# Routing from the unnormed residual: logits scaled afterwards, the first task's rows gathered raw, the stored rows normed by GpSimd

## What is computed

```
h2 = rmsnorm(xs, norm2_g[l]) * (1.0 + sc2) + sh2
xs = xs + g2 * channel_mixer(h2, l, ...)

# channel mixer of layer 1
logits = (h @ w_router[i]).astype(F32)
top_v, top_i = lax.top_k(logits, TOP_K)
top_w = jax.nn.softmax(top_v, axis=-1)
gates = jnp.sum(jax.nn.one_hot(top_i, N_EXP) * top_w[..., None], axis=-2)
for e in range(N_EXP):
    y = y + gates[..., e:e + 1] * swiglu(h, w_ex_gate[i, e], w_ex_up[i, e], w_ex_down[i, e])
```

## Time and profile before

| | us |
|---|---|
| median of three runs | 1532.15 (1530.58 to 1533.17) |
| the profiled execution | 1533.48 |
| its span, first to last instruction | 1531.4 |

### The profile page before, as it was taken

One profiled execution on the slowest core, in us unless ns is written; L12 is line 12 of the kernel. 1 busy time (PEld: TensorE's weight loads), 2 busy tenths in 40 slices (PEclk: granted clock), 3 DMA queues, 4 the chain that ended last, 5 costly groups with the idle time before them and its releaser, 6 DMA issues.

```text
span 1531.4 us, 22089 instructions
## 1 busy us (share of the span) xinstructions
PE 1484.0 (97%) x8652; PEld 1308.3 (85%) x8652; DVE 937.7 (61%) x1077; ACT 786.7 (51%) x896; POOL 53.6 (4%) x54
## 2 busy tenths in 40 slices
PE   5999999999999999999999999998999999999997
PEld 4788969799899999997889696998888888888875
DVE  3542265555554254346522755556798898988988
ACT  4434354453432242235333544435778778787875
POOL 0100000000000000001000000000000000000002
PEclk8999999999999999999999999999999999999999
DMA  9754365467753544265333554535899999999994
GB/s 329 245 179 152 110 221 165 157 205 244 261 154 96 150 130 126 90 220 169 121 116 111 165 165 138 165 121 186 298 376 389 376 374 374 381 386 376 376 378 165
DMA packets 236026, 342.33 MB, mean 224 GB/s; under 512 B 8629, under 2 KB 156766, under 8 KB 235694
## 3 DMA queue, kind: packets, MB, share of 16 engines
q1 hardware_dynamic: 227392, 313.32, 59.9%
q0 software_dynamic: 6496, 24.69, 4.4%
q10 hardware_dynamic: 2062, 3.24, 0.6%
HBM read 325.74 MB, written 15.47 MB: 223 GB/s over the span
## 4 chain that ended last, share of the span: by engine, by line
PE 89%; DVE 5%; ACT 3%; DMA 1%; issue 1%; ACTq 0%; DVEq 0%; SPq 0%
PE ps L689 26%; PE ps L691 25%; PE ps L690 25%; PE ps L706 2%; DVE wlo L2142 2%; PE ps L887 1%; PE ps L921 1%; PE ps L905 1%; ACT whi L1575 1%; PE ps L1119 1%; PE ps L748 1%; ACT ebuf L1483 1%; PE ps L785 1%; PE ps L716 1%; DMA raw<-in_w_ada_dram 0%
## 5 line engine op out<-in xcount | busy, mean ns | idle before, releaser
L689 PE MATMUL ps<-hhi,whi 128*128 128x384 f32 x824 | 276.6, 336 | 0.3 <-DVE hidlo L2239 0.3
L691 PE MATMUL ps<-hhi,wlo 128*128 128x384 f32 x824 | 275.3, 334 | 0.0
L690 PE MATMUL ps<-hlo,whi 128*128 128x384 f32 x824 | 275.3, 334 | 0.0
L1763 DVE TENSOR_TENSOR wlo<-raw,whi 128x2048 fp32r<-128x2048 f32 x66 | 151.0, 2289 | 179.9 <-ACT whi L1317 168.3
L2142 DVE TENSOR_TENSOR wlo<-raw,whi 128x2048 fp32r<-128x2048 f32 (+1 forms) x81 | 179.0, 2227 | 27.4 <-ACT whi L1575 26.9
L1575 ACT ACTIVATE whi<-raw 128x2048 fp32r<-128x2048 f32 (+1 forms) x81 | 150.5, 1868 | 49.4 <-PE ps L691 47.8
L2142 DVE TENSOR_TENSOR wlo<-mraw,whi 128x2048 fp32r<-128x2048 f32 (+2 forms) x81 | 160.7, 1992 | 18.1 <-ACT whi L1575 17.6
L689 PE MATMUL ps<-whi,xgh 128*128 128x512 f32 (+1 forms) x432 | 164.7, 381 | 6.2 <-DVE wlo L2142 3.7
L1575 ACT ACTIVATE whi<-mraw 128x2048 fp32r<-128x2048 f32 (+2 forms) x81 | 136.6, 1686 | 53.2 <-PE ps L691 52.9
L691 PE MATMUL ps<-whi,xgl 128*128 128x512 f32 (+1 forms) x432 | 161.4, 374 | 0.0
L690 PE MATMUL ps<-wlo,xgh 128*128 128x512 f32 (+1 forms) x432 | 161.3, 373 | 0.0
(11 more groups left out here) (343 smaller groups left out, 2498.2 us busy)
## 6 DMA issues: line engine op xcount, KB each, us to landing
raw<-in_w_ada_dram SPq DMA_DIRECT2D x64, 512.0 KB, 5.4
raw<-in_w_ex_up_dram SPq DMA_DIRECT2D x27, 1024.0 KB, 6.7
raw<-in_w_ex_down_dram SPq DMA_DIRECT2D x27, 1024.0 KB, 5.1
raw<-in_w_gate_dram SPq DMA_DIRECT2D x48, 512.0 KB, 4.6
raw<-in_w_in_dram SPq DMA_DIRECT2D x44, 512.0 KB, 5.9
raw<-in_w_ex_gate_dram SPq DMA_DIRECT2D x18, 1024.0 KB, 7.3
mraw<-in_w_ex_gate_dram SPq DMA_DIRECT2D x18, 1024.0 KB, 7.8
mraw<-in_w_ex_down_dram SPq DMA_DIRECT2D x18, 1024.0 KB, 8.6
```

Of the source, the lines that this page charges most:

```text
L689: pe.matmul(out, s[0], m[0], start=first, stop=False, **kw)
L690: pe.matmul(out, s[0], m[1], start=False, stop=False, **kw)
L691: return pe.matmul(out, s[1], m[0], start=False, stop=last, **kw)
L1763: dve.tensor_tensor(wlo[:, n % RING, :], raw[:, n % RING, :], whi[:, n % RING, :].bitcast(F32), ALU.subtract).then_inc(lo_done, 1)
```

## The change

Six things change; the sums stay the same up to rounding.

1. The logits. In the output projection VectorE multiplies the router's weights by the modulation's scale, once for each kind of token (`wr2`). TensorE multiplies the residual `xT` with them as soon as its channel groups are there (`raw_logits`), and sums the squares between. The reciprocal root `rcol` is applied to the turned logits by VectorE, which also adds the shift's part (`shlog`). That part is made by 16 matmuls in front of the third slot of the output projection.
2. `mean_squares(3)`, `root(3)` in its old place, `normalise(3)` and `modulate(3)` are gone: neither the spreading of the root nor `macc` is made.
3. TensorE turns the residual (`residual_turned`) behind the logits and ahead of the places of the tokens; the turning of `macc` (L1079), its copies (L1740) and ScalarE's store (L1743) are gone.
4. `first_rows` gathers from `xtok2`, with `gat` holding rcol instead of 1; block 0 goes to PSUM banks of its own. One more matmul spreads which slots hold context tokens (`prompt`).
5. ScalarE scales and shifts the gathered rows as latent ones (`hmod`), VectorE adds the context rows with their scale and the difference of the shifts (`first_modulated`); high and low parts are made from `hmod`.
6. GpSimd makes the normed rows for the later tasks from `xtok2` by nine instructions of 128x1024 (times rcol, times scale, plus shift) and stores them to `h2d`. Scale and shift rows reach it as the gate's do: four more transposes, one more copy and store (`modrow`, `m2d`), four more broadcast loads. ScalarE's wait for this store is now in `expert_task`, in front of the copy to `ehh`.

The core of the diff:

```diff
@@ gpsimd
+            pool.wait_ge(rows_in, 16 * 7)
+            pool.wait_ge(rstd_ready, 2 * DEPTH)
+            pool.wait_ge(x2_tr, BLK)
+            for b in range(BLK):
+                v = int(b == 0)
+                pool.wait_ge(x2_ev, b + 1)
+                pool.tensor_scalar(h2tok[:, b, :], xtok2[:, b, :], rcol[:, 1, b:b + 1], None, ALU.mult).then_inc(h2_rows, 1)
+                pool.wait_ge(h2_rows, 3 * b + 1)
+                pool.tensor_tensor(h2tok[:, b, :], h2tok[:, b, :], murow[:, v, :], ALU.mult).then_inc(h2_rows, 1)
+                pool.wait_ge(h2_rows, 3 * b + 2)
+                pool.tensor_tensor(h2tok[:, b, :], h2tok[:, b, :], shrow[:, v, :], ALU.add).then_inc(h2_rows, 1)
+            pool.wait_ge(h2_rows, 3 * BLK)
+            pool.dma_start(h2d.rearrange("(b p) d -> p b d", p=P), h2tok[:, :, :]).then_inc(h2_out, 16)
@@ tensor: out_projection, in front of the third slot
+                            pe.transpose(ps[0:KD, 6, v * P:(v + 1) * P], mods[:, 1, SH2:SH2 + KD, v], ident)
+                            pe.transpose(ps[0:KD, 6, (2 + v) * P:(3 + v) * P], amul[:, 1, 1, :, v], ident)
                             mm = pe.transpose(ps[0:KD, 7, v * P:(v + 1) * P], mods[:, 1, G2:G2 + KD, v], ident)
                         mm.then_inc(g2_tr, 1)
+                        pe.wait_ge(wrout_in, 16)
+                        for v in range(2):
+                            for k in range(KD):
+                                mm = pe.matmul(ps[:, 5, v * N_EXP:(v + 1) * N_EXP],
+                                               mods[:, 1, SH2 + k, v:v + 1].to_broadcast([P, P]), wrout[:, k, 0:N_EXP],
+                                               start=(k == 0), stop=(k == KD - 1))
+                        mm.then_inc(sh_mm, 1)
@@ tensor: router
+                def raw_logits(k):
                     g = 32 * (k % 4)
-                    mm = pe.matmul(ps[g:g + 32, 7, 0:T], wrout[:, k, :], macc[:, k, :], start=(k < 4), stop=(k >= 4),
-                                   tile_position=(0, g))
+                    for v, t in ((0, slice(P, T)), (1, slice(0, P))):
+                        mm = pe.matmul(ps[g:g + 32, 7, t], wr2[:, v, k, :], xT[:, k, t], start=(k < 4 and v == 0),
+                                       stop=(k >= 4 and v == 1),
+                                       tile_position=(0, g))
+                    return mm
...
+                for k in range(6):
+                    raw_logits(k)
+                pe.wait_ge(wr2_ready, 2)
+                pe.wait_ge(sqs_done, SQS[3])
+                squares_part(0, False)
+                pe.wait_ge(res_done, 15)
+                raw_logits(6)
+                pe.wait_ge(sq_done, SQ0[3] + 4)
+                squares_part(1, False)
+                pe.wait_ge(res_done, 16)
+                raw_logits(7).then_inc(rt_rows, 1)
+                pe.wait_ge(sq_done, SQ0[3] + 5)
+                squares_part(2, True).then_inc(ssq_done, 1)
...
+                pe.wait_ge(rstd_ready, 2 * DEPTH)
                 for b in range(BLK):
-                    pe.wait_ge(x2_ev, b + 1)
...
+                    residual_turned(b)
@@ tensor: first_rows
-                pe.wait_ge(h2_ev, BLK)
+                pe.wait_ge(x2_ev, BLK)
+                pe.matmul(ps[:, 4, 0:P], ones[:, :], prompt[:, :], start=True, stop=True)
@@ scalar: expert_task, experts
+                        act.wait_ge(h2_out, 16)
                         act.activation(ehh[:, 4 * c:4 * c + CHUNKS[c] // P, :].rearrange("p k c -> p (k c)"),
...
-                act.wait_ge(h2_out, 16)
                 for h in range(2):
                     act.wait_ge((half_rows, xg_tr)[h], 1)
+                    for k in range(4 * h, 4 * h + 4):
+                        act.activation(hmod[:, k, :], ps[:, 2 + h, (k % 4) * P:(k % 4 + 1) * P], ACT.Identity,
+                                       scale=amul[:, 1, 1, k, 0:1], bias=mods[:, 1, SH2 + k, 0:1]).then_inc(half_mod, 1)
@@ vector: router
+                for b in range(BLK):
+                    x = dve.scalar_tensor_tensor(lg[:, b, :], ps[:, 7, T + b * N_EXP:T + (b + 1) * N_EXP], rcol[:, 1, b:b + 1],
+                                                 shlog[:, int(b == 0), :], ALU.mult, ALU.add)
...
+                dve.tensor_scalar(prompt[:, :], slot1[:, :], posx[:, 0, 0:1], None, ALU.is_equal)
                 for b in range(BLK):
-                    x = dve.tensor_scalar(gat[:, b, :], slotc[:, P:2 * P], 1.0, posx[:, b, 0:1], ALU.add, ALU.is_equal)
+                    x = dve.tensor_scalar(gat[:, b, :], slot1[:, :], posx[:, b, 0:1], rcol[:, 1, b:b + 1], ALU.is_equal, ALU.mult)
...
+                first_modulated(0)
...
-                for h in range(2):
-                    first_low(h)
+                first_low(0)
+                first_modulated(1)
+                first_low(1)
...
+            def first_modulated(h):
+                dve.wait_ge(half_mod, 4 * h + 4)
+                ks = range(4 * h, 4 * h + 4)
+                for k in ks:
+                    x = dve.scalar_tensor_tensor(hmod[:, k, :], ps[:, h, (k % 4) * P:(k % 4 + 1) * P], amul[:, 1, 1, k, 1:2],
+                                                 hmod[:, k, :], ALU.mult, ALU.add)
+                link(x)
+                for k in ks:
+                    x = dve.scalar_tensor_tensor(hmod[:, k, :], ps[:, 4, 0:P], shdiff[:, k:k + 1], hmod[:, k, :], ALU.mult, ALU.add)
+                x.then_inc(h_mod, 1)
```

More of the change, by code:

```diff
@@ L254, in prefix_step_kernel @@
         gat = at("gat", T, oraw_at + 4096, shape=[BLK, P])
+        slot1 = at("slot1", P, oraw_at + 2048)
+        prompt = at("prompt", P, oraw_at + 2560)
+        shlog = at("shlog", 2 * N_EXP, oraw_at + 3072, shape=[2, N_EXP])
+        shdiff = at("shdiff", KD, oraw_at + 3200)
         ehh = at("ehh", KF * P, oraw_at + 5632, F32R, [KF, P])
@@ L1060, in router, with squares_part @@
             def router():
-                pe.wait_ge(wrout_in, 16)
-                for k in range(KD):
-                    if k % 2 == 0:
-                        pe.wait_ge(chain_m, 8 * 3 + k + 2)
-                        pe.wait_ge(mod_done, 4 * 3 + k // 2 + 1)
-                    g = 32 * (k % 4)
-                    mm = pe.matmul(ps[g:g + 32, 7, 0:T], wrout[:, k, :], macc[:, k, :], start=(k < 4), stop=(k >= 4),
-                                   tile_position=(0, g))
-                mm.then_inc(rt_rows, 1)
+                def raw_logits(k):
+                    g = 32 * (k % 4)
+                    for v, t in ((0, slice(P, T)), (1, slice(0, P))):
[3 more added lines that the diff above has]
+                    return mm
+                def squares_part(n, last):
+                    for b in range(BLK):
+                        part = (ssum[:, 0, :], macc[:, 6, :], macc[:, 7, :])[n]
+                        mm = pe.matmul(ps[:, sum_bank(3) + b, 0:1], part[:, b * P:(b + 1) * P], ones[:, 0:1], start=(n == 0),
+                                       stop=last)
+                    return mm
+                pe.wait_ge(wr2_ready, 1)
+                pe.wait_ge(g2_ready, 2)
+                pe.wait_ge(res_done, 14)
+                for k in range(6):
[11 more added lines that the diff above has]
+                squares_part(2, True).then_inc(ssq_done, 1)
                 pe.wait_ge(lrow_ready, 1)
@@ L1074, in router @@
                 mm.then_inc(rt_done, 1)
+                pe.wait_ge(rstd_ready, 2 * DEPTH)
                 for b in range(BLK):
-                    pe.wait_ge(x2_ev, b + 1)
-                    for k in range(KD):
-                        mm = pe.transpose(ps[:, 2 * b + k // 4, (k % 4) * P:(k % 4 + 1) * P],
-                                          macc[:, k, b * P:(b + 1) * P], ident)
-                    mm.then_inc(h2_tr, 1)
+                    residual_turned(b)
                 pe.wait_ge(sel_ready, 1)
@@ L1092, in first_rows @@
                 pe.wait_ge(gat_ready, 1)
-                pe.wait_ge(h2_ev, BLK)
+                pe.wait_ge(x2_ev, BLK)
+                pe.matmul(ps[:, 4, 0:P], ones[:, :], prompt[:, :], start=True, stop=True)
                 for k in range(KD):
                     for b in range(BLK):
-                        mm = pe.matmul(ps[:, 2 + k // 4, (k % 4) * P:(k % 4 + 1) * P], h2tok[:, b, k * P:(k + 1) * P],
-                                       gat[:, b, :], start=(b == 0), stop=(b == BLK - 1))
+                        mm = pe.matmul(ps[:, (2 if b else 0) + k // 4, (k % 4) * P:(k % 4 + 1) * P],
+                                       xtok2[:, b, k * P:(k + 1) * P], gat[:, b, :], start=(b < 2), stop=(b != 1))
                     if k == 3:
@@ L1295, in _ @@
                 out_projection(l)
-                mean_squares(2 * l + 1)
                 if l == 0:
+                    mean_squares(1)
                     units()
@@ L1369, in modulate @@
                 for p in range(4):
-                    if i == 3 and p < 2:
-                        residual_turned(p)
                     if i == 0:
```

(11 more changed lines are left out.)

76 lines of the change are left out of this document (43 added, 33 removed).

## The result

The changed kernel is slower: 1545.78 us (four runs, 1542.46 to 1546.87) against 1532.23 of the kernel before on the same chip, a ratio of 1.0083 with a 95% interval of 1.0065 to 1.0101, thus +10 to +15.5 us. The forecast was 1540.9. In the profiled execution the span is 1543.0 against 1531.4, +11.6.

The account below looks back on a forecast made before the run. TensorE, busy 97% of the span, was taken to bound the kernel. Projection +5.8 and first expert matmul +2.9 (-3.9 without GpSimd's blocking) gave +8.7 us on 1532.15, thus 1540.9; range 1529 to 1546.

Parts of the forecast that it names:

- case A: Router to first expert matmul: GpSimd's reads and VectorE's second SBUF read exclude each other; 1536.5 to 1545 us, chance 0.52.
- part 1: Output projection: added transposes and small matmuls cost 4.1 us, a clock drop 1.7; together 5.8, ends 4.1 and 7.5.
- parts 2 and 3: Last projection matmul to first expert matmul, GpSimd's effect left out: early logits and raw gather bring it 3.9 us earlier.
- part 4: Normed rows on GpSimd: nine instructions take 14 us and block VectorE, turning -3.9 us at the first expert matmul into +2.9.
- the gather's terms: First rows' gather: 5.62 us, plus 0.2 for one more matmul, plus 1.0 for half clock and waiting; ends at 1066.8.
- the full case: VectorE's chain to the task table ends only when GpSimd does; first expert matmul at 1077.3, +2.9 us.
- Part 2: Router: logits without the norm are turned 8.4 us earlier; gat is ready 6.4 us earlier.
- the transposes' clock: 24 residual transposes ahead of the position matmuls: taken as 4.3 us at mostly half clock, where full clock gives 2.8.
- Part 3: Rows gathered raw: store leaves the path, a tail is added; first expert matmul at 1070.5, 3.9 us earlier.
- the tail: Gather's end to first expert matmul: scalings, additions, copy and low half take 3.7 us, where before needed 2.6.
- Cases B and C: B: GpSimd disturbs nothing, +1.9 us, chance 0.28. C: TensorE decides, faster by 2.5 to 4 us, chance 0.12.
- case D: Expert task: GpSimd so slow that stored rows come after ScalarE's new wait; 1548 us, chance 0.08.

Follow-up runs that it names:

- e1: Changed kernel without GpSimd's nine instructions; raw rows stored, so later tasks lack norm, scale and shift. Ratio 1.0013 to the kernel before.
- e11: Changed kernel without GpSimd's arithmetic (later tasks' rows not normed) and with one matmul for the shift. Ratio 0.9983 to the kernel before.
- e6: Changed kernel with one matmul for the shift's logits, after VectorE's sums, in place of 16 small ones. Ratio 1.0030 to the kernel before.
- e5: Changed kernel with GpSimd's nine instructions replaced by 24 chained memsets; later tasks get constants. Ratio 1.0032 to the kernel before.
- e10: Changed kernel with all nine GpSimd instructions of the one-input kind; later tasks lack scale and shift. Ratio 1.0037 to the kernel before.
- e4: Changed kernel with GpSimd's nine instructions started only when the task table is there. Ratio 1.0084 to the kernel before.
- e12: Changed kernel with one shift matmul, norm's scale on ScalarE, six GpSimd instructions behind the task table, some ScalarE and VectorE work later. Ratio 1.0039 to before.
- e2: Kernel before with only the change's 4 transposes and 16 small matmuls added in the last output projection, results unused. Ratio 1.0014.
- e3: Kernel before with nine GpSimd instructions of the change's shapes added, writing a buffer nobody reads before the end. Ratio 1.0052.

## Why the prediction was right, and where it was only right in the sum

The side and the mechanism (case A) held. The sum came out of two errors that partly cancel, and that it stayed in the range is luck: 1545.78 is above the 1545 at which I had ended case A and 0.22 below the end of the whole range, 1546. Forecast and measured, in us, the latter by the stretches of after, before and e1:

| step | forecast | measured |
|---|---|---|
| part 1, projection | +5.8 | +5.66 |
| parts 2 and 3, B to C without GpSimd | -3.9 | -5.97 |
| part 4, GpSimd on VectorE | +6.8 | +12.05 |
| sum | +8.7 | +11.7 |

The split between the last two rows holds for the clock that e1 had. With e11 and e6, where the transposes ran in part at half clock, the same rows are -3.1 and +5.8.

Two sums of the prediction are off by a little: the gather's terms give 1066.6 and not 1066.8, and the terms of the full case 1077.0 and not 1077.3. The forecast would have been +8.4 us.

- Part 1. The 32 records took 3.65 us (3.6 forecast) and four transposes 0.44. The clock fell for 3.4 us. In two other profiles (e1, e5) it fell for 6.8, the upper end, 24.1 us from A to B, and in e10 not at all, 21.0.
- Part 2. Logits turned 8.1 us earlier than before, counted from B (8.4 forecast). The step that failed is the transposes' clock: 2.84 us at full clock, not 4.3 (e6 and e11 have 4.50). By e1, `gat` was ready 7.3 us earlier, and not 6.4.
- Part 3. The gather ran at full clock in e1 (5.52), where 1.0 was kept for half; the tail was 3.69 from its end to C, as forecast (3.7). In after it ran in part at half clock (7.15, mean granted 0.76), but that was hidden, for VectorE came to the rows only at 1077.6. The second half cost nothing: C to end is 456.9 in e1.
- Part 4. The mis-sized term is GpSimd's length. A two-input instruction took 2.36 us where 1.85 was my upper end, and the one-input 2.85 where I took 0.97. A memset of 128 columns was no measure for an instruction that reads. With 23.1 us instead of 14, the shape of the estimate was wrong as well: the task table was ready with the end of the sixth instruction (1077.6), not of the ninth, and the last two only held `posq` and `xgl`. C came 32.9 us behind B, where 29.7 were forecast, though GpSimd ended 8 us later than forecast.
- I had counted on instructions with two SBUF inputs alone. `gat`, L2123 and L2125 have one, and were held as well (1.58, 2.29 and 2.19 us). Not always: in e6 `gat` lay beside GpSimd's first one-input record (1061.11 to 1063.96) and took its 0.85.
- Cases B and C are excluded by after's records, case D too: the store was issued at 1085.5, and ScalarE's `ehh` (L1647, the successor of L1596) ran at 1106.35 with no idle time before it.

The Trainium skill, "SBUF — State Buffer", Who interferes with whom, lists what this trace shows beyond my forecast: casts and one-tensor scalar instructions of VectorE can contend with GpSimd, two-input ones only with a GpSimd instruction that reads, and a reduction never. The runs agree: beside memsets only the former were held, and the reduction L2133 took 0.53 us beside L690, as in e1. They disagree in one point. The Trainium skill, same section, has the one that comes second wait for the whole instruction, but beside the one-input L688 (1069.90 to 1072.74) VectorE's L2113 ended at 1071.15 and four two-input ones (L2114 to L2119, 0.27 to 0.28 us each) ran free behind it. (The expectation for e10 says nine; two of the others are reductions, the rest came later.)

For GpSimd's two-input kind the trace has 2.34 to 2.42 us. The Trainium skill, "GPSIMD Engine Reference", Performance versus the Vector engine, gives 4497 ns for 2048 columns, thus 2.25 us for 1024, an estimate, which was nearer than my bound.

## What to carry to other kernels

Before work is given to an idle GpSimd, count the VectorE instructions that would run beside it, and not GpSimd's microseconds: each short one in a dependent chain can wait out a whole GpSimd instruction of 2.4 us, so a chain of 0.2 us steps beside a few long two-input instructions is the worst place for them. The cost is the sum of the links that are held less what VectorE would have waited anyway, so the same nine cost 12.05, 8.3 and 5.8 us in three kernels. Moving them elsewhere helps only where VectorE has slack, and e4 and e12 show that the instruction after which TensorE starts isn't where VectorE's work stops mattering. Tiny matmuls in a full TensorE stretch cost that stretch their own time (4.1 us here, transposes included) and up to 3.2 more in clock, of which less than half reached the end in e2: sum on another engine first and use one matmul.

## What the hardware showed that I had not expected

- GpSimd with one SBUF input and a column of scalars took 2.85 us for 128x1024, more than with two SBUF inputs (2.36); a memset of that size took 1.0 (24 in 24.3 us). But the one-input kind disturbs VectorE least of the reading ones: 27.0 us of it cost some 1 us up to C.
- VectorE's instructions with one input in PSUM and one in the SBUF were not held: four additions into `hmod` took 1.13 us beside GpSimd and without it.
- The blocking goes both ways: GpSimd's one-input instruction took 7.00 us beside weight splits (e4), and the two-input one 4.16 (e3).
- The granted clock falls at different places from one kernel to the next. In part at half clock the 24 transposes cost 1.7 us more and the gather 1.6, and that alone took more than half of what e11 should have won.
